# Second attention's head norm: two tiles' squares summed at once in two column groups, inverse roots held as two rounded parts

## Chip, cores and metric

The kernel runs on one core of a Trainium2 chip. The metric is the device time of one execution in microseconds (us); three executions of the kernel before are given with their median.

## What is computed

Two transformer blocks in sequence over 512 tokens and 16 meta tokens (528 rows) of width 1024, in fp32. The first block (gated delta rule, short convolution, gated feed-forward) is not touched. The second has two layers: sparse attention with an MLP, then the attention that the change is in (`fox_attention`) with an MLP. That attention needs keys, values and forget gates from one normalization of the residual and queries from another, and each head (64 wide, 16 heads) of the keys and of the queries is normalized by itself:

```python
def rms_norm(x, g):
    xf = x.astype(jnp.float32)
    y = xf * lax.rsqrt(jnp.mean(xf * xf, axis=-1, keepdims=True) + EPS)
    return (y * g.astype(jnp.float32)).astype(x.dtype)

def shared_kv(h, w_kv, f_bias, k_gain):
    k, v, fl = jnp.split(h @ w_kv, [B_W, 2 * B_W], axis=-1)
    k = rms_norm(k.reshape(B, T, B_HEADS, HEAD_DIM), k_gain)
    v = v.reshape(B, T, B_HEADS, HEAD_DIM)
    log_f = jax.nn.log_sigmoid(fl.astype(jnp.float32) + f_bias.astype(jnp.float32))
    c = jnp.cumsum(log_f, axis=1).transpose(0, 2, 1)
    ...
def fox_attention(h, w_q, q_gain, w_out, k, v, c):
    q = rms_norm((h @ w_q).reshape(B, T, B_HEADS, HEAD_DIM), q_gain)
    ...
```

## The kernel before

Data lie with features on the partitions: a tile is 128 features (two heads) by 528 tokens, so 8 tiles hold the keys and 8 the queries. Products with fp32 weights are made from two rounded parts of each operand (hi and lo, both fp32r): hi x hi, hi x lo, lo x hi. A **block** is one output tile: its weights are 128 x 1024 floats, loaded by SyncE's queue, split into hi by ScalarE (`split_hi`, L474) and lo by GpSimd (`split_lo`, L482), and multiplied on TensorE (`products`, L518) in 48 products, 3 parts x 8 rows of tiles x 2 halves of 264 tokens. Weight slots and PSUM accumulators are double: the weights of block j+1 are split while block j is multiplied, once block j-1 is done, and block j+2 may start when block j has been evicted.

The stage is written out by hand, one function for each engine (`pe_fox`, `act_fox`, `dve_fox`, `pool_fox`), each a loop over 25 blocks j; what stands in the code behind block j runs behind it in that engine's queue. Engines meet at semaphores: `f_sq` (squares made), `f_used` (sums made), `f_root`, `f_inv`, `f_spread`, `f_app` (tile normalized), `acc_free` (block evicted), `block_done` (block multiplied).

- Block 0 gives the forget gates, blocks 1 to 8 the keys (tiles 0 to 7), 9 to 16 the queries (tiles 8 to 15), 17 to 24 the values.
- VectorE evicts block j (L2651, times the row norm) and, for j < 8, makes one lo part of the second normalized input (`low`, L789) and one step of the forget-gate series (`dve_forget`, L2584 to L2621).
- ScalarE splits weights, squares tile n behind block j = n+2 (`square`, L2540, into one of two buffers `fox_sq`), and takes the roots of eight tiles' sums at j=10 and j=18 (`roots`, L2544).
- TensorE sums the squares of tile n behind block n+2 (`sums`, L2476): a product with a window of 16 columns that puts the two heads' sums into rows 2m and 2m+1 of PSUM and adds zero to the others, in fp32, for the two halves of the tokens.
- VectorE inverts the roots of eight tiles (`inverse`, L2630, in rows 0 to 15 of the otherwise zero `fox_inv`).
- TensorE spreads a tile's two rows over 128 partitions (`spreads`, L2485), in fp32 with a 0/1 matrix `fox_spread`: tiles 0 to 7 in blocks 11 to 14 and tiles 8 to 15 in blocks 19 to 22, an even one in the middle of a block (`midway`) and the odd one behind it.
- VectorE normalizes the tile with the result (`apply`, L2636). `spreads(n)` waits until tile n-1 has been normalized.

Behind the stage runs the attention. Three of its TensorE lines serve for comparison in what follows: L2250 (`scores`), L2282 (`turn`, a transposition, over all columns) and L2315 (`values`), where an fp32 product with 64 weight columns goes in turn to PSUM partitions 0 to 63 and 64 to 127:

```python
for hh in range(2):
    col = (p if fox else p // 4) * P + 64 * hh
    n = ROWS[kb + x]
    at2 = (hh * nk + x) * rows
    mm = pe.matmul(ps[64 * hh:64 * hh + 64, VALUE_BANK + t // 4, at:at + rows],
                   v[0:n, kb + x, col:col + 64], ptr[TURN["turn", j, i] % 4][0:n, at2:at2 + rows],
                   start=(kb + x == 0), stop=(kb + x == t))
```

Of the kernel before, what the change touches and what calls it, by code (L numbers as in the profile page):

```python
# [17 lines left out]
F32 = mybir.dt.float32  # L18
F32R = mybir.dt.float32r
BF16 = mybir.dt.bfloat16  # L20
ALU = mybir.AluOpType
ACT = mybir.ActivationFunctionType
AX = mybir.AxisListType

P = 128
# [3 lines left out]
T = NMETA + SEQ  # L29
HT = T // 2  # L30
# [26 lines left out]
def num(b):  # L57
    return b.c + 2 * b.i
# [56 lines left out]
def wait(e, sem, value):  # L115

    if isinstance(value, int) and value <= 0:
        return
    e.wait_ge(sem, value)
# [32 lines left out]
def build_program(nc, io):  # L152
# [9 lines left out]
    def region(start):  # L162
        pos = [start]

        def sb(name, shape, dt=F32):
            n = 2 if dt == BF16 else 4
            for s in shape[1:]:
                n *= s
            n = -(-n // 32) * 32
            off = pos[0]  # L170
            pos[0] += n
            return place(name, shape, dt, off)

        sb.pos = pos
        return sb
# [11 lines left out]
    ident = keep("ident", [P, P])  # L187
    ones = keep("ones", [P, P])
    win128 = keep("win128", [P, 31])
    win64 = keep("win64", [P, 30])  # L190
# [3 lines left out]
    eps = keep("eps", [P, 1])  # L194
# [98 lines left out]
    assert r2.pos[0] <= nc.sbuf_usable_end, r2.pos[0]  # L293
    rf = region(phase_at + 8 * F)
    fox_sq = [rf(f"fox_sq{u}", [P, T]) for u in range(2)]
    fox_root = rf("fox_root", [16, T])
    fox_inv = rf("fox_inv", [P, T])
    fox_spread = rf("fox_spread", [P, 8 * P])
    assert rf.pos[0] <= phase_at + 16 * F
    rs = region(phase_at + 24 * F)  # L300
    fox_sp = [rs(f"fox_sp{i}", [16, T]) for i in range(5)]
# [2 lines left out]
    bias = rdsa("bias", [C, NCH, T])  # L304
# [36 lines left out]
    ps = nc.alloc_psum_tensor("ps", [P, 8, 512], F32)  # L341
# [27 lines left out]
    def both(name):  # L369
# [23 lines left out]
    f_sq, f_used, f_root, f_inv, f_spread, f_app = map(sem, (  # L393
        "fox_square", "fox_square_used", "fox_root", "fox_inverse", "fox_spread", "fox_normalized"))
# [29 lines left out]
    def pair_of(b, rows=P):  # L424

        return ps[0:rows, b:b + 2, 0:HT]

    def two(ap):
        return ap.rearrange("p (h t) -> p h t", h=2)
# [9 lines left out]
    def tile_at(buf, m, n=T, off=0):  # L439
        step = TS if buf is qkv or buf is oacc else T  # L440
        return buf[:, bass.ds(m * step + off, n)]
# [111 lines left out]
    def stage_at(u):  # L553
        return stage[:, u * T:(u + 1) * T]
# [1912 lines left out]

    def pe_fox(pe):

        def sums(n):  # L2470
            m = n % 8
            pe.wait_ge(f_sq, n + 1)
            if n == 8:
                pe.wait_ge(f_root, 1)
            for h in range(2):
                mm = pe.matmul(ps[0:16, 4 + h, 0:HT], win64[:, 14 - 2 * m:30 - 2 * m],  # L2476
                               fox_sq[n % 2][:, h * HT:(h + 1) * HT], start=(m == 0), stop=(m == 7))
            mm.then_inc(f_used, 1)

        def spreads(n):  # L2480
            m = n % 8
            pe.wait_ge(f_inv, n // 8 + 1)
            wait(pe, f_app, n)
            for h in range(2):
                mm = pe.matmul(ps[:, 6 + h, 0:HT], fox_spread[:, m * P:(m + 1) * P], fox_inv[:, h * HT:(h + 1) * HT],  # L2485
                               start=True, stop=True)
            mm.then_inc(f_spread, 1)

        for j in range(25):
            x = (xbh, xbl) if 9 <= j <= 16 else (xah, xal)  # L2490
            first = dict(fresh=4, sums=pe_sums()) if j == 0 else dict(fresh=5) if j == 9 else {}
            n = 2 * (j - 11) if 11 <= j <= 14 else 8 + 2 * (j - 19) if 19 <= j <= 22 else None
            if n is not None:
                first["midway"] = lambda pe: spreads(n)
            products(pe, Blk(FOX + j, 0), *x, KT, **first)
            if j == 1:
                pe.wait_ge(acc_free, FOX + 1)
                for c in range(NCH):
                    mm = pe.matmul(ps[0:ROWS[c], 7, c:c + 1], rstd[0:1, c * C:ENDS[c]], ones[0:1, 0:1],
                                   start=True, stop=True)  # L2500
                mm.then_inc(f_turn, 1)
            if 2 <= j <= 17:
                sums(j - 2)
            if n is not None:
                spreads(n + 1)
            if j >= 18:
                fox_values(pe, j - 18)
# [25 lines left out]
    def act_fox(act):  # L2533
        root = act_root()

        def square(n):
            m = n % 8
            act.wait_ge(acc_free, FOX + n + 2)
            wait(act, f_used, n - 1)
            act.activation(fox_sq[n % 2][:, :], tile_at(pf, m if n < 8 else 16 + m), ACT.Square).then_inc(f_sq, 1)  # L2540

        def roots(i):
            act.wait_ge(f_used, 8 * (i + 1))
            act.activation(two(fox_root[:, :]), pair_of(4, 16), ACT.Sqrt, bias=eps[0:16, 0:1], scale=1.0 / 64  # L2544
                           ).then_inc(f_root, 1)

        def raw(m):
            b = Blk(FOX + 17 + m, 0)
            act.wait_ge(block_done, num(b) + 1)
            act.wait_ge(acc_free, num(b))  # L2550
            act.activation(two(stage_at(m % 2)), acc(b), ACT.Copy).then_inc(acc_free, 1)

        for j in range(25):
            split_hi(act, Blk(FOX + j + 1, 0))
            if j == 0:
                root(act)
            if j < 8:
                split_residual(act, j, 6, xbh, False)
            if j == 2:
                act.wait_ge(f_turn, 1)  # L2560
                act.activation(fox_tok[:, 0:4], ps[0:C, 7, 0:4], ACT.Copy)
                act.activation(fox_tok[0:ROWS[4], 4:5], ps[0:ROWS[4], 7, 4:5], ACT.Copy)
                act.wait_ge(sp_abs, 2)
                act.activation(fox_sp[0][:, :], lfneg[:, :], ACT.Abs)
                act.drain()
                act.activation(fox_sp[1][:, :], fox_sp[0][:, :], ACT.Exp, scale=-1.0).then_inc(sp_exp, 1)
            if 2 <= j <= 17:
                if j == 10:
                    roots(0)
                square(j - 2)  # L2570
            if j == 18:
                roots(1)
            if j >= 18:
                raw(j - 18)
            if j >= 19:
                store(act, j - 19)
            if j == 19:
                act.activation(rowvec[0:1, 7:8], eps[0:1, 0:1], ACT.Exp)
        raw(7)
# [44 lines left out]
    def dve_fox(dve):  # L2624
        root, low, forget = dve_root(), lows(5, 6, xbh, xbl), dve_forget(dve)

        def inverse(i):
            wait(dve, f_spread, 8 * i)
            dve.wait_ge(f_root, i + 1)
            dve.reciprocal(fox_inv[0:16, :], fox_root[:, :]).then_inc(f_inv, 1)  # L2630

        def apply(n):
            x = tile_at(pf, n if n < 8 else 8 + n)
            k = 3 if n < 8 else 4
            dve.wait_ge(f_spread, n + 1)
            dve.scalar_tensor_tensor(two(x), two(x), headgain[:, k:k + 1], pair_of(6), ALU.mult, ALU.mult  # L2636
                                     ).then_inc(f_app, 1)

        for j in range(17):
            b = Blk(FOX + j, 0)  # L2640
            if j == 0:
                root(dve)
            dve.drain()
            dve.wait_ge(block_done, num(b) + 1)
            dve.wait_ge(acc_free, num(b))
            if j == 0:
                dve.tensor_tensor(two(lfneg[:, :]), acc(b, 16), two(rstd[0:16, :]), ALU.mult).then_inc(acc_free, 1)
                dve.drain()
            else:
                x = tile_at(pf, j - 1 if j < 9 else j + 7)  # L2650
                dve.tensor_tensor(two(x), acc(b), two(rstd[:, :]), ALU.mult).then_inc(acc_free, 1)  # L2651
            if j < 8:
                low(dve, j)
                next(forget)
            if j == 8:
                dve.memset(fox_inv[:, :], 0.0)
                dve.tensor_copy(fox_spread[:, :].rearrange("p (k n) -> p k n", n=64),
                                ident[:, 0:16].unsqueeze(2).broadcast_to([P, 16, 64]))
                dve.drain()
            if j == 9:  # L2660
                inverse(0)
            if j == 10:
                apply(0)
            if 11 <= j <= 14:
                apply(2 * (j - 11) + 1)
                if j < 14:
                    apply(2 * (j - 11) + 2)
        inverse(1)
        for n in range(8, 16):
            apply(n)  # L2670
# [348 lines left out]
```

## Times and profile before

| | us |
|---|---|
| three executions | 2874.48, 2880.0, 2881.43 |
| median | 2880.0 |
| the profiled execution | 2881.1 |
| its span, first to last instruction | 2879.1 |
| TensorE busy in the span | 2684.5 (93%) |
| VectorE, ScalarE, GpSimd busy | 1389.8, 1019.5, 1085.3 |
| mean granted TensorE clock | 0.966 |

The profile comes from one execution. It has one record for each instruction; an fp32 matmul has two TensorE records, an fp32r matmul one. TensorE's records overlap, since they last until a result has left the array: how much time an instruction takes of the engine is read from the distance of the starts, not from its duration. The stage of the change lies between about 2170 and 2344 us.

### The profile page before, as it was taken

What the parts mean: (1) busy time and instruction counts of PE and PEld (TensorE: products, weight loads), DVE (VectorE), ACT (ScalarE), POOL (GpSimd) and SP (SyncE); (2) the same over time, 40 slices, a digit from 0 to 9 for tenths busy, and PEclk for the clock granted to TensorE, in tenths of its full rate; (3) what the DMA queues carried; (4) which work ended last, traced back from release to release, by engine and by line L of the source; (5) the groups of instructions that cost most, each with busy time, mean ns of one, the idle gap of its engine ahead of it and who ended that gap; (6) DMA issues with size and microseconds to landing.
All of it is one profiled execution on the core that took longest, in us unless ns stands there. A gap on an engine that the chain in (4) does not pass through costs nothing.

```text
span 2879.1 us, 48582 instructions
## 1 busy us (share of the span) xinstructions
PE 2684.5 (93%) x17811; PEld 2317.2 (80%) x17811; DVE 1389.8 (48%) x2068; ACT 1019.5 (35%) x1763; POOL 1085.3 (38%) x564
## 2 busy tenths in 40 slices
PE   6985887889999999999889899999999999999998
PEld 6974887868987778888778669999998886777876
DVE  2664566633212663233678656354367224545432
ACT  4772222233244242222523574222233256422222
POOL 3421333314444434444446214444444311444443
PEclk8997888899999999999999999999999999999999
DMA  2210000012222233223211002222222210223322
GB/s 97 91 55 6 12 10 11 13 60 88 90 92 95 88 96 95 93 90 95 95 52 54 21 2 81 88 88 90 91 88 74 66 45 2 68 94 95 95 88 94
DMA packets 88891, 197.91 MB, mean 69 GB/s; under 512 B 38172, under 2 KB 40270, under 8 KB 88760
## 3 DMA queue, kind: packets, MB, share of 16 engines
q1 hardware_dynamic: 84964, 192.72, 21.7%
q10 hardware_dynamic: 3796, 3.38, 0.4%
q8 instruction: 89, 1.46, 0.2%
q14 instruction: 42, 0.34, 0.0%
HBM read 192.24 MB, written 3.82 MB: 68 GB/s over the span
## 4 chain that ended last, share of the span: by engine, by line
issue 53%; POOL 13%; PE 5%; POOLq 3%; DVE 3%; DVEq 1%; ACT 1%; ACTq 0%
POOL wl L482 12%; PE ps L518 3%; POOLq L2220 2%; DVE work L2123 1%; DVE top L2120 1%; PE ps L1876 1%; POOL xbl L2229 1%; POOLq L130 0%; POOLq L2228 0%; POOLq L2217 0%; PE ps L881 0%; PE ps L893 0%; PE ps L2250 0%; DVEq L619 0%; DVEq L2121 0%
## 5 line engine op out<-in xcount | busy, mean ns | idle before, releaser
L482 POOL TENSOR_TENSOR wl<-wraw,wh 128x1024 fp32r<-128x1024 f32 x353 | 876.1, 2482 | 1210.6 <-ACT wh L474 1210.5
L474 ACT ACTIVATE wh<-wraw 128x1024 fp32r<-128x1024 f32 x353 | 372.5, 1055 | 575.6 <-PE ps L518 487.6
L518 PE MATMUL ps<-xah,wh 128*128 128x264 f32 (+1 forms) x2672 | 500.2, 328 | 25.3 <-ACT xah L847 14.2
L518 PE MATMUL ps<-xah,wl 128*128 128x264 f32 (+1 forms) x2672 | 488.0, 323 | 0.0
L518 PE MATMUL ps<-xal,wh 128*128 128x264 f32 (+1 forms) x2672 | 486.2, 322 | 0.0
L518 PEld LDWEIGHTS ps<-xah,wh 128*128 128x128 f32 x2672 | 405.4, 189 | 79.5 <-issue 23.3
L518 PEld LDWEIGHTS ps<-xah,wl 128*128 128x128 f32 x2672 | 403.8, 189 | 41.4 <-issue 0.8
L518 PEld LDWEIGHTS ps<-xal,wh 128*128 128x128 f32 x2672 | 401.7, 188 | 40.7
L666 DVE TENSOR_TENSOR res<-res,stage 128x512 f32 (+3 forms) x112 | 81.9, 731 | 442.0 <-ACT stage L582 442.0
L518 PE MATMUL ps<-xbh,wh 128*128 128x264 f32 (+1 forms) x1392 | 274.0, 337 | 13.6 <-POOL wl L482 13.0
L518 PE MATMUL ps<-xbh,wl 128*128 128x264 f32 (+1 forms) x1392 | 269.5, 333 | 0.0
L518 PE MATMUL ps<-xbl,wh 128*128 128x264 f32 (+1 forms) x1392 | 269.5, 333 | 0.0
L518 PEld LDWEIGHTS ps<-xbh,wh 128*128 128x128 f32 x1392 | 217.4, 188 | 48.7 <-POOL wl L482 16.5
L582 ACT ACTIVATE stage<-ps 128x512 f32<-128x512 f32 (+1 forms) x136 | 81.9, 602 | 460.8 <-PE ps L518 460.8
L518 PEld LDWEIGHTS ps<-xbl,wh 128*128 128x128 f32 x1392 | 217.5, 188 | 27.4
L518 PEld LDWEIGHTS ps<-xbh,wl 128*128 128x128 f32 x1392 | 217.4, 188 | 27.4
L659 DVE TENSOR_SCALAR xbh<-stage 128x512 f32 (+3 forms) x102 | 147.6, 1447 | 18.2 <-issue 16.6
L661 DVE TENSOR_TENSOR xbl<-stage,xbh 128x512 f32 (+3 forms) x102 | 114.5, 1122 | 15.2 <-issue 1.0
L2406 DVE TENSOR_REDUCE rowmax<-ps 106x2 f32<-106x212 f32 (+2 forms) x96 | 68.0, 708 | 85.3 <-PE ps L2262 40.5
L2227 POOL CAST xbh<-ofull 128x528 fp32r<-128x528 f32 x16 | 10.0, 623 | 220.5 <-DVE ofull L2441 220.5
L1392 POOL TENSOR_TENSOR qkm<-qkm,tri 106x424 f32<-106x424 f32 x20 | 19.8, 1011 | 180.7 <-DVE qkm L1511 180.7
L2250 PE MATMUL ps<-pf 64*106 64x212 f32 (+5 forms) x384 | 69.1, 438 | 12.8 <-DVEq L418 8.9
(347 smaller groups left out, 3089.0 us busy)
## 6 DMA issues: line engine op xcount, KB each, us to landing
wraw<-in_w SPq DMA_DIRECT2D x353, 512.0 KB, 3.5
res<-in_x SPq DMA_DIRECT2D x4, 528.0 KB, 5.6
res<-in_x ACTq DMA_DIRECT2D x1, 2048.0 KB, 7.8
out<-res SPq DMA_DIRECT2D x1, 2048.0 KB, 6.9
block_in<-mt SPq DMA_DIRECT2D x120, 4.0 KB
xq<-block_out SPq DMA_DIRECT2D x120, 8.0 KB
block_out<-yy SPq DMA_DIRECT2D x20, 56.0 KB
cossin<-in_cossin ACTq DMA_DIRECT2D x1, 528.0 KB
```

What stands on the lines that cost most here:

```text
L474: act.activation(wh[:, s * DM:(s + 1) * DM], wraw[:, s * DM:(s + 1) * DM], ACT.Copy).then_inc(hi_done, 1)
L482: pool.tensor_tensor(wl[:, s * DM:(s + 1) * DM], wraw[:, s * DM:(s + 1) * DM], wh[:, s * DM:(s + 1) * DM].bitcast(F32), ALU.subtract).then ...
L518: mm = pe.matmul(ps[:, 2 * s + h, 0:width], ws[:, s * DM + kk * P:s * DM + (kk + 1) * P], x[:, at:at + width], start=(h not in [o[0] for o ...
L582: act.activation(shaped(out(j, u), live), acc(b, live=live), func, **more).then_inc(acc_free, 1)
L659: dve.tensor_scalar(hi, x, 1.0, None, ALU.mult)
L661: return dve.tensor_tensor(lo, x, hi.bitcast(F32), ALU.subtract)
L666: return dve.tensor_tensor(r, r, live_stage(u) if live else stage_at(u), ALU.add)
L1876: mm = pe.matmul(ps[0:ROWS[t], 4 + 2 * (n % 2) + x, 0:c], ix_zero[:, 2 * (m % 2) + hh, C * t:ENDS[t]], pf[:, 16 * T + o:16 * T + o + c], s ...
L2120: dve.max(top8[0:ROWS[t], 8 * t:8 * t + 8], work_of(t))
L2220: pool.drain()
L2250: pe.matmul(ps[0:rows, b + hh, 0:hi - lo], pf[half, q0:q0 + rows], pf[half, k0 + lo:k0 + hi], start=True, stop=False)
L2406: most = dve.tensor_reduce(rowmax[0:rows, n, 1 if k == LAST4 else 0, :], ps[0:rows, b:b + 2, 0:hi - lo], AX.X, ALU.max, negate=True)
```

## The change

Squares are summed for two tiles at once, behind every second block (j = 3, 5, ..., 17): tile 2p into PSUM partitions 0 to 31 and tile 2p+1 into partitions 32 to 63, with a window `fox_win` that is 32 columns wide (the old one, widened by 16 zero columns). Roots and inverses then take 64 rows, of which 16 carry sums. The inverse is kept in two fp32r parts, rounded in rows 0 to 63 and the rest in rows 64 to 127 of `fox_inv`; `fox_spread` becomes an fp32r 0/1 matrix that picks both parts of a head's row, so that one fp32r product spreads a tile's inverses. `square(n)` waits for the sums of the pair before its own.

```diff
+    fox_root = rf("fox_root", [64, T])
+    fox_inv = rf("fox_inv", [P, T], F32R)
+    fox_spread = rf("fox_spread", [P, 8 * P], F32R)
+    fox_win = rf("fox_win", [P, 46])
...
-        def sums(n):
-            m = n % 8
-            pe.wait_ge(f_sq, n + 1)
-            if n == 8:
+        def sums(pair):
+            m = pair % 4
+            pe.wait_ge(f_sq, 2 * pair + 2)
+            if pair == 4:
                 pe.wait_ge(f_root, 1)
             for h in range(2):
-                mm = pe.matmul(ps[0:16, 4 + h, 0:HT], win64[:, 14 - 2 * m:30 - 2 * m],
-                               fox_sq[n % 2][:, h * HT:(h + 1) * HT], start=(m == 0), stop=(m == 7))
+                for u in range(2):
+                    mm = pe.matmul(ps[32 * u:32 * u + 32, 4 + h, 0:HT], fox_win[:, 14 - 2 * m:46 - 2 * m],
+                                   fox_sq[u][:, h * HT:(h + 1) * HT], start=(m == 0), stop=(m == 3))
             mm.then_inc(f_used, 1)
...
-            if 2 <= j <= 17:
-                sums(j - 2)
+            if 2 <= j <= 17 and j % 2:
+                sums((j - 3) // 2)
...
         def square(n):
-            wait(act, f_used, n - 1)
+            wait(act, f_used, n // 2)
...
         def roots(i):
-            act.wait_ge(f_used, 8 * (i + 1))
-            act.activation(two(fox_root[:, :]), pair_of(4, 16), ACT.Sqrt, bias=eps[0:16, 0:1], scale=1.0 / 64
+            act.wait_ge(f_used, 4 * (i + 1))
+            act.activation(two(fox_root[:, :]), pair_of(4, 64), ACT.Sqrt, bias=eps[0:64, 0:1], scale=1.0 / 64
...
         def inverse(i):
-            dve.reciprocal(fox_inv[0:16, :], fox_root[:, :]).then_inc(f_inv, 1)
+            dve.reciprocal(fox_root[:, :], fox_root[:, :])
+            dve.drain()
+            dve.tensor_copy(fox_inv[0:64, :], fox_root[:, :])
+            dve.drain()
+            dve.tensor_tensor(fox_inv[64:128, :], fox_root[:, :], fox_inv[0:64, :].bitcast(F32), ALU.subtract
+                              ).then_inc(f_inv, 1)
...
             if j == 0:
                 root(dve)
+                dve.memset(fox_win[:, 30:46], 0.0)
+                dve.tensor_copy(fox_win[:, 0:30], win64[:, :])
...
             if j == 8:
-                dve.memset(fox_inv[:, :], 0.0)
-                dve.tensor_copy(fox_spread[:, :].rearrange("p (k n) -> p k n", n=64),
-                                ident[:, 0:16].unsqueeze(2).broadcast_to([P, 16, 64]))
+                picks = fox_spread[:, :].rearrange("p (m u k n) -> p u m k n", u=2, k=2, n=64)
+                for u in range(2):
+                    hi, lo = (ident[:, at:at + 8].rearrange("p (m k) -> p m k", k=2).unsqueeze(3).broadcast_to(
+                        [P, 4, 2, 64]) for at in (32 * u, 64 + 32 * u))
+                    dve.tensor_tensor(picks[:, u, :, :, :], hi, lo, ALU.add)
                 dve.drain()
```

TensorE's queue behind blocks 3 and 4, before (`win` is the 16-column window, `xah`, `xal`, `wh` and `wl` the hi and lo parts of input and weights):

```order
L518 MATMUL ps<-xal,wh 128x264 x8
L2476 MATMUL ps<-fox_sq_165,win_61 16x264 [waits fox_square]
L2476 MATMUL ps<-fox_sq_165,win_61 16x264
L518 MATMUL ps<-xah,wh 128x264 [waits acc_free,lo_done]
L518 MATMUL ps<-xah,wh 128x264 x7
L518 MATMUL ps<-xah,wl 128x264 x8
L518 MATMUL ps<-xal,wh 128x264 x8
L518 MATMUL ps<-xah,wh 128x264 x8
L518 MATMUL ps<-xah,wl 128x264 x8
L518 MATMUL ps<-xal,wh 128x264 x8
L2476 MATMUL ps<-fox_sq_164,win_61 16x264 [waits fox_square]
L2476 MATMUL ps<-fox_sq_164,win_61 16x264
```

and the same place now, where line numbers are those of the changed kernel (L519 is the products, L2478 the sums):

```order
L519 MATMUL ps<-xal,wh 128x264 x8
L2478 MATMUL ps<-fox_sq_164,fox_win 32x264 [waits fox_square]
L2478 MATMUL ps<-fox_sq_165,fox_win 32x264
L2478 MATMUL ps<-fox_sq_164,fox_win 32x264
L2478 MATMUL ps<-fox_sq_165,fox_win 32x264
L519 MATMUL ps<-xah,wh 128x264 [waits acc_free,lo_done]
L519 MATMUL ps<-xah,wh 128x264 x7
L519 MATMUL ps<-xah,wl 128x264 x8
L519 MATMUL ps<-xal,wh 128x264 x8
L519 MATMUL ps<-xah,wh 128x264 x8
L519 MATMUL ps<-xah,wl 128x264 x8
L519 MATMUL ps<-xal,wh 128x264 x8
```

Two matmuls behind each block became four behind every second, alternating between the buffers and so between the column groups; behind block 4 the next block follows at once.

VectorE's queue from the eviction of block 8 (the first row) to the first `apply`, before:

```order
L2651 TENSOR_TENSOR pf<-ps,rstd 128x528 [waits acc_free,block_done]
L2656 MEMSET fox_inv 128x528
L2657 COPY fox_spread<-ident 128x1024
L2651 TENSOR_TENSOR pf<-ps,rstd 128x528 [waits acc_free,block_done]
L2630 RECIPROCAL fox_inv<-fox_root 16x528 [waits fox_root]
L2651 TENSOR_TENSOR pf<-ps,rstd 128x528 [waits acc_free,block_done]
L2636 SCALAR_TENSOR_TENSOR pf<-pf,headgain,ps 128x528 [waits fox_spread]
```

and now:

```order
L2660 TENSOR_TENSOR pf<-ps,rstd 128x528 [waits acc_free,block_done]
L2669 TENSOR_TENSOR fox_spread<-ident 128x4x128 x2
L2660 TENSOR_TENSOR pf<-ps,rstd 128x528 [waits acc_free,block_done]
L2632 RECIPROCAL fox_root<-fox_root 64x528 [waits fox_root]
L2634 CAST fox_inv<-fox_root 64x528
L2636 TENSOR_TENSOR fox_inv<-fox_root,fox_inv 64x528
L2660 TENSOR_TENSOR pf<-ps,rstd 128x528 [waits acc_free,block_done]
L2643 SCALAR_TENSOR_TENSOR pf<-pf,headgain,ps 128x528 [waits fox_spread]
```

The fill and the copy became two additions, and between the reciprocal and block 10's eviction stand two more instructions.

## Rows read from the trace of the kernel before

**Rows 1.** The page, parts 1 and 2: busy time, granted clock by slice.

```profile
PE 2684.5 (93%) x17811; PEld 2317.2 (80%) x17811; DVE 1389.8 (48%) x2068; ACT 1019.5 (35%) x1763; POOL 1085.3 (38%) x564
...
PEclk8997888899999999999999999999999999999999
```

**Rows 2.** The stage: length, busy PE, PEld, DVE, ACT, POOL (instructions), clock, DMA.

```profile
2172.50:2344.00 171.50, 171.50 (x1270) 155.90 (x1270) 64.55 (x66) 54.20 (x92) 63.08 (x27) 1.00 0.23 72
```

**Rows 3.** Timeline of TensorE, two plain blocks' first products (start, duration, instruction).

```profile
2131.18 1.15 PE L518 MATMUL ps<-xbh,wh 128*128 128x264 f32 x8
...
2137.02 1.15 PE L518 MATMUL ps<-xbh,wh 128*128 128x264 f32 x8
```

**Rows 4.** Timeline around the first two tiles' sums.

```profile
2177.93 1.13 PE L518 MATMUL ps<-xal,wh 128*128 128x264 f32 x8
...
2178.99 1.06 PE L2476 MATMUL ps<-fox_sq,win 128*16 128x264 f32 x4
2179.10 0.71 DVE L2651 TENSOR_TENSOR pf<-ps,rstd 128x528 f32<-128x528 f32 x1 [5.23 <-PE ps L518]
...
2180.75 0.63 ACT L2540 ACTIVATE fox_sq<-pf 128x528 f32<-128x528 f32 x1
...
2186.11 0.71 DVE L2651 TENSOR_TENSOR pf<-ps,rstd 128x528 f32<-128x528 f32 x1 [2.53 <-PE ps L518]
```

**Rows 5.** Groups of instructions from 2170 to 2340: sums and spreads.

```profile
L2485 PE MATMUL ps<-fox_inv,fox_spread 128*128 128x264 f32 x64 | 17.3, 392 | 0.0
...
L2476 PE MATMUL ps<-fox_sq,win 128*16 128x264 f32 x64 | 17.0, 389 | 0.0
```

**Rows 6.** Timeline of TensorE in the attention, then a cut of it.

```profile
2355.30 1.50 PE L2315 MATMUL ps<-ptr,vtok 106*64 106x106 f32 x28
...
2357.33 0.70 PE L2282 MATMUL ps<-ident,prob 104*106 104x104 f32 x6
...
2355.30 0.31 PE L2315 MATMUL ps<-ptr,vtok 106*64 106x106 f32 x2
```

**Rows 7.** Timeline of VectorE, evictions of blocks 11 and 14.

```profile
2243.17 0.71 DVE L2651 TENSOR_TENSOR pf<-ps,rstd 128x528 f32<-128x528 f32 x1 [2.15 <-PE ps L518]
...
2269.60 0.71 DVE L2651 TENSOR_TENSOR pf<-ps,rstd 128x528 f32<-128x528 f32 x1 [2.15 <-PE ps L518]
```

**Rows 8.** Timeline of VectorE from block 4's eviction to block 8's, one GpSimd row.

```profile
2193.12 0.71 DVE L2651 TENSOR_TENSOR pf<-ps,rstd 128x528 f32<-128x528 f32 x1 [2.10 <-PE ps L518]
...
2201.37 2.58 POOL L482 TENSOR_TENSOR wl<-wraw,wh 128x1024 fp32r<-128x1024 f32 x1 [3.82 <-ACT wh L474]
...
2201.79 4.27 DVE L2605 SCALAR_TENSOR_TENSOR fox_sp<-fox_sp,fox_sp 16x528 f32<-16x528 f32 x3
2207.19 0.71 DVE L2651 TENSOR_TENSOR pf<-ps,rstd 128x528 f32<-128x528 f32 x1 [1.14 <-PE ps L518]
...
2219.31 0.42 DVE L2618 CAST decay_row<-lfneg 16x528 bf16<-16x528 f32 x1
2219.81 0.70 DVE L2621 TENSOR_TENSOR lfneg<-lfneg,decay_row 16x528 f32<-16x528 f32 x1
...
2222.47 0.71 DVE L2651 TENSOR_TENSOR pf<-ps,rstd 128x528 f32<-128x528 f32 x1 [0.19 <-issue]
```

**Rows 9.** Timeline: preparation of the spread, both inversions, and the spreads behind them.

```profile
2223.24 0.50 DVE L2656 MEMSET fox_inv<- 128x528 f32 x1
2223.65 1.75 DVE L2657 COPY fox_spread<-ident 128x1024 f32<-128x1024 f32 x1
2228.25 0.71 DVE L2651 TENSOR_TENSOR pf<-ps,rstd 128x528 f32<-128x528 f32 x1 [2.85 <-PE ps L518]
2231.40 3.44 DVE L2630 RECIPROCAL fox_inv<-fox_root 16x528 f32<-16x528 f32 x1 [2.45 <-ACT fox_root L2544]
...
2239.17 1.05 PE L2485 MATMUL ps<-fox_inv,fox_spread 128*128 128x264 f32 x4
...
2293.41 3.44 DVE L2630 RECIPROCAL fox_inv<-fox_root 16x528 f32<-16x528 f32 x1 [8.11 <-ACT fox_root L2544]
2301.92 1.05 PE L2485 MATMUL ps<-fox_inv,fox_spread 128*128 128x264 f32 x4
```

More of the change, by code:

```diff
@@ L295, in build_program @@
     fox_sq = [rf(f"fox_sq{u}", [P, T]) for u in range(2)]
-    fox_root = rf("fox_root", [16, T])
-    fox_inv = rf("fox_inv", [P, T])
-    fox_spread = rf("fox_spread", [P, 8 * P])
+    fox_root = rf("fox_root", [64, T])
+    fox_inv = rf("fox_inv", [P, T], F32R)
+    fox_spread = rf("fox_spread", [P, 8 * P], F32R)
+    fox_win = rf("fox_win", [P, 46])
     assert rf.pos[0] <= phase_at + 16 * F
```

## The prediction

> **What bounds the kernel now.** I read the page's first two parts, then the stage that the change touches. TensorE is busy for 93% of the span and the granted clock is 9 tenths or more from the ninth slice on, so a stage is judged by whether TensorE ever waits in it [rows 1]. In the second attention's projections (2172.5 to 2344.0) it never does: 171.50 us busy of 171.50, granted clock 1.00 (that is 2.4 GHz), while VectorE works 64.55, ScalarE 54.20 and GpSimd 63.08 us there [rows 2]. So every microsecond that leaves TensorE's queue in this stage leaves the stage, as long as the other engines keep up with shorter blocks; and a microsecond added on VectorE costs nothing until something on TensorE waits for it.
>
> The unit of the stage is one weight block: 48 one-pass products. Two blocks with nothing else between them follow each other in 5.84 us (first products at 2131.18 and 2137.02), which is 0.122 us a product [rows 3].
>
> **The sums.** From j=2 to 17 each block is followed by one tile's sums. The evictions, which start when a block's products end, are then 7.01 us apart (2179.10, 2186.11) [rows 4]: a tile's sums cost 7.01 - 5.84 = 1.17 us, sixteen of them 18.7. Four records make them up, two passes for each of the two fp32 matmuls (64 records for 32 matmuls [rows 5]); 0.89 of the 1.17 is these four passes at 0.22 each, and 0.28 is paid once for the group. The gap ahead of it shows: the eight products from 2177.93 should be through at 2177.93 + 8 x 0.122 = 2178.90, and the sums begin at 2178.99 [rows 4].
> The change issues the same 32 matmuls, but four at a time, every second block (the order above). If the two column groups work side by side, a pair of tiles costs four slots of 0.22 and one 0.28, say 1.18 with the stagger. The trace of before has a witness: L2315 in the attention writes PSUM partitions 0 to 63 and 64 to 127 in turn, with 106 rows of weights (all four row groups), in fp32. There two records start in the same hundredth of a microsecond, and 28 records of 106 columns are through between 2355.30 and about 2356.6, 0.047 us each, where L2282, also fp32 and 106 columns but over the full width, needs (0.70 - 0.25) / 5 = 0.09 each [rows 6]. Full overlap, then, for 64-column groups. I take it for 32-column ones too. Gain: 8 x (2 x 1.17 - 1.18) = **9.3 us**. The other bound is no overlap: eight passes of 0.22 plus 0.28 is 2.06 a pair, a gain of 8 x 0.28 = 2.2 us.
> The Trainium skill ("TensorEngine Tiling (Array Packing)", Tiling Modes, Key Properties) says that a change of tiling mode drains the array but a change of tile within a mode does not; by this rule the drain is paid at both ends of each group, eight groups where there were sixteen, and not between the two column groups, so the sum would be mine. The 0.09 us gap of rows 4 agrees with the first half, the twin starts of rows 6 with the second.
>
> **The spreads.** Between the evictions of blocks 11 and 14 lie three stretches of (2269.60 - 2243.17) / 3 = 8.81 us, each with one block, one tile's sums and two spreads [rows 7]. A spread costs (8.81 - 5.84 - 1.17) / 2 = 0.90 us: again four records of 0.22 for two fp32 matmuls [rows 5]. As fp32r operands each half is one pass over 128 weight columns and 264 moving ones, exactly the shape and type of the products: 2 x 0.122 = 0.24. Sixteen spreads save 16 x 0.66 = **10.5 us**. The bounds are close here; both ends are rows of this stage.
>
> **VectorE's new work.** (a) `fox_win` at j=0: a fill and a 30-column copy, each under the 0.50 us of the fill of `fox_inv` [rows 9], since both touch far less. Behind them queues only block 0's eviction, for which TensorE waits behind block 1. Nothing, at most 0.5 us. (b) At j=8 the 0.50 fill and 1.75 copy go (the copy took 1.75 because it began while GpSimd was at work) and two adds of 128x512 come, about 0.70 each like any two-input operation [rows 8, 9]. Nothing. (c) `inverse`: after the 3.44 us reciprocal come a conversion (about 0.42, the nearest being the cast) and a subtraction (about 0.70) [rows 8, 9], with drains 1.3 us. With block 9 ending at 2228.15 (its eviction starts at 2228.25) the reciprocal ended at 2234.84 and the first spread came at 2239.17: 4.3 us of slack [rows 9]. Now the first spread comes 1.17 + 5.84 + 2.92 = 9.93 us after block 9, as block 10 has no sums any more, and the inverse is ready 6.69 + 1.3 = 8.0 after it. 1.9 us of cover remain; nothing is paid, and if this cover fails TensorE waits at j=11's midway. The second `inverse` ended at 2296.85 for a spread at 2301.92; 3.8 us remain [rows 9]. Nothing.
> (d) Block 10's eviction queues behind the longer inverse by about 1 us; only block 12 needs the bank. Nothing.
>
> **Where cover gets thin.** The forget-gate series runs on VectorE between the evictions. From the eviction of block 4 (2193.12) to that of block 8 (2222.47) pass 29.35 us, of which only 1.14 and 0.19 are idle [rows 8]: 28.0 us of work. TensorE took 28.04 for these four blocks and will take 4 x 5.84 + 2 x 1.18 = 25.7. VectorE reaches block 8's eviction 2.3 us late, ends it 3.0 late, and the square takes 0.63 more [rows 4]. The pair sums need it 5.84 after block 8's end: 2.2 us to spare. Evictions and weight splits have a block of slack more. So **nothing** is charged.
>
> **Sum.** 9.3 + 10.5 = 19.8 us. Made against the profiled execution it is 2881.1 - 19.8 = 2861.3; the runs' median lies 1.1 us under that execution, and the forecast is for a median: 2880.0 - 19.8 = **2860.2 us**. After the stage everything shifts as one, since weights are fetched only two blocks ahead.
>
> **Rivals.**
> *The columns don't overlap* (only the spreads gain in full): 10.5 + 2.2 = 12.7, time 2867.3. For it: 32-column groups with two 128-row moving streams of 264 columns appear nowhere in this trace. Against: rows 6. Chance 0.09.
> *VectorE comes late.* A two-input operation that starts while GpSimd subtracts waits for its end: L2621 takes 0.70, and three L2605 of the same size took 4.27 instead of 2.1 with a GpSimd subtraction under way from 2201.37 to 2203.95 [rows 8]. One such wait (2.1 us) already falls in most iterations; with blocks of 5.84 us and a VectorE that lags, a second one can fall into j=5, 6 or 7 or on `inverse`'s subtraction. Two more would eat the 2.2 us and stall the fourth pair of sums by about 2; one on `inverse` stalls the first spread by 1.3. Time 2860.2 + 2 to 4 = 2862 to 2864. Chance 0.14. The Trainium skill ("SBUF — State Buffer", Who interferes with whom) states it as a rule, that the one who comes second blocks fully; by it every late iteration risks a whole GpSimd instruction, and the time is that of this rival. The stretched L2605 agrees with the rule.
> *Each change of column group costs what the group's edges cost* (slower than before). The passes of rows 6 alternate between the groups, so a pair of tiles has seven changes. If each cost 0.28 and nothing overlapped, that is 56 x 0.28 = 15.7 us against the 12.7 gained: 2883.0. It is slower than before from 0.23 us a change, by over 0.3% from 0.38. Rows 6 show changes at under 0.01 us; only 32 columns behaving unlike 64 would bring it. Chance 0.02.
> *The spread keeps its two passes.* Then only 9.3 are gained, 2870.7. The products' 0.122 us with the same type speaks against it. Chance 0.03.
>
> **How the numbers follow.** Forecast 0.70; the remaining 0.02 is for a cause that I don't see, on either side. Likeliest: 2860.2. The runs of before reach from 5.5 under to 1.4 over their median, so the forecast alone spans 2854.7 to 2861.6; the late VectorE reaches 2864 and the missing overlap 2867.3 + 1.4. Range 2854.5 to 2868.7. A measurement of this kernel tells a change of 0.3% or 8.6 us from none: faster is below 2871.4, which all cases but the third rival and the unseen cause meet. Faster 0.94, same 0.04, slower 0.02.
>
> **What would show it.** Right: 32 spread records instead of 64, about 0.12 us apart; sum records starting in twos; evictions after blocks with sums 7.0 us behind the last and after blocks without 5.84; at block 14's eviction (2269.60 before) a lead of 12 x 1.17 - 6 x 1.18 + 7 x 0.66 = 11.6 us; TensorE still without idle time in the stage, which ends near 2324. Wrong: sum groups of 2 us; an idle stretch ahead of the sums of j=9 or the spread of j=11; a granted clock under 1.00 anywhere in the stage; or a stage 20 us shorter with the end not 20 us earlier, which would mean the attention behind it had waited for something else.

## The result and the profile after

The change takes 2858.4 us (median of 4 runs, 2856.6 to 2859.7) against 2880.2 us before (4 runs in the same comparison, 2874.5 to 2881.4). The ratio is 0.9928 with a 95% interval of 0.9911 to 0.9945. That is 21.7 us less, where 19.8 were forecast. The granted clock of the page is the share of TensorE's full clock, 2.4 GHz, that it got.

The page of the changed kernel, parts 1 and 2, beside [rows 1]:

```profile
span 2854.8 us, 48528 instructions
...
PE 2655.9 (93%) x17779; PEld 2299.2 (81%) x17779; DVE 1393.1 (49%) x2074; ACT 1020.1 (36%) x1763; POOL 1084.5 (38%) x564
...
PEclk8997888999999999999999999999999999999999
```

TensorE has 32 instructions fewer: sixteen spreads of four records became sixteen of two. VectorE has 6 more.

The whole span can't size the effect, since it is 24.3 us shorter here. So I measured the stage by itself, from the reciprocal of the row norm on VectorE, with which it opens, to the first fill of the row sums, with which the attention behind it begins. First the two ends before:

```profile
2166.24 3.45 DVE L761 RECIPROCAL rstd<-rstd 128x528 f32<-128x528 f32 x1 [2.05 <-ACT rstd L744]
...
2344.11 0.08 DVE L2445 MEMSET rowsum<- 106x24 f32 x1 [12.03 <-PE ps L518]
```

and after, with the new preparation of the window between them:

```profile
2161.66 3.45 DVE L762 RECIPROCAL rstd<-rstd 128x528 f32<-128x528 f32 x1 [2.05 <-ACT rstd L745]
2165.22 0.50 DVE L2651 COPY fox_win<-win 128x30 f32<-128x30 f32 x1
2165.22 0.07 DVE L2650 MEMSET fox_win<- 128x16 f32 x1
2165.89 0.69 DVE L2656 TENSOR_TENSOR lfneg<-ps,rstd 16x528 f32<-16x528 f32 x1 [0.17 <-issue]
...
2319.65 0.08 DVE L2446 MEMSET rowsum<- 106x24 f32 x1 [12.05 <-PE ps L519]
```

The stage shrank from 177.87 to 158.00 us, by **19.87**. Behind it the two executions agree within 0.2 us (535.0 and 535.1 to the end). The other 4.6 us of the span had been won before the stage opened (2166.24 against 2161.66), in code that both kernels share. The expectations below speak of the stage from block 0's eviction, 173.8 and 153.8 us; that measure makes the gain 0.2 larger (20.07), because the eviction itself starts 0.2 later behind the reciprocal. The table further down has both.

How the stage runs now, in VectorE's timeline (evictions of blocks 2 to 4 and 11 to 14, beside [rows 4] and [rows 7]):

```profile
2174.53 0.71 DVE L2660 TENSOR_TENSOR pf<-ps,rstd 128x528 f32<-128x528 f32 x1 [2.88 <-PE ps L519]
...
2180.36 0.71 DVE L2660 TENSOR_TENSOR pf<-ps,rstd 128x528 f32<-128x528 f32 x1 [1.35 <-PE ps L519]
...
2187.42 0.71 DVE L2660 TENSOR_TENSOR pf<-ps,rstd 128x528 f32<-128x528 f32 x1 [2.14 <-PE ps L519]
...
2232.06 0.71 DVE L2660 TENSOR_TENSOR pf<-ps,rstd 128x528 f32<-128x528 f32 x1 [2.15 <-PE ps L519]
...
2239.57 0.71 DVE L2660 TENSOR_TENSOR pf<-ps,rstd 128x528 f32<-128x528 f32 x1 [2.15 <-PE ps L519]
...
2245.88 0.71 DVE L2660 TENSOR_TENSOR pf<-ps,rstd 128x528 f32<-128x528 f32 x1 [2.15 <-PE ps L519]
...
2253.40 0.71 DVE L2660 TENSOR_TENSOR pf<-ps,rstd 128x528 f32<-128x528 f32 x1 [2.15 <-PE ps L519]
```

Between blocks 2 and 3 there are no sums: 5.83 us. Between 3 and 4 there is a pair's: 7.06. Farther on, a stretch with a pair's sums and two spreads is 7.51 and one with two spreads alone 6.31, where each was 8.81. A spread thus costs (6.31 - 5.84) / 2 = 0.24 us, and a pair's sums 1.20. At block 14's eviction the lead over the kernel before, counted from the opening of the stage, is (2269.60 - 2166.24) - (2253.40 - 2161.66) = 11.6 us, as forecast. TensorE's own timeline shows both kinds:

```profile
2180.26 1.08 PE L2478 MATMUL ps<-fox_sq,fox_win 128*32 128x264 f32 x8
2181.27 1.24 PE L519 MATMUL ps<-xah,wh 128*128 128x264 f32 x8
...
2228.71 0.40 PE L2487 MATMUL ps<-fox_inv,fox_spread 128*128 128x264 f32 x2
2228.95 1.13 PE L519 MATMUL ps<-xbh,wh 128*128 128x264 f32 x8
```

Eight records of sums take 1.01 us to the next block's start, as long as four did in [rows 4] (2178.99 to 2179.98). The two column groups overlap in full. Two spread records take 0.24.

### The profile page after: what moved, and what is told of

It reads as the page before. It is cut to its first block, busy times and chain, and to the rows that moved or that the text cites. A ratio compares the mean times of both kernels' runs of the same rounds, so it can differ in the third digit from the quotient of the medians.

```text
span 2854.8 us, 48528 instructions
## 1 busy us (share of the span) xinstructions
PE 2655.9 (93%) x17779; PEld 2299.2 (81%) x17779; DVE 1393.1 (49%) x2074; ACT 1020.1 (36%) x1763; POOL 1084.5 (38%) x564
## 4 chain that ended last, share of the span: by engine, by line
issue 53%; POOL 13%; PE 5%; POOLq 3%; DVE 3%; DVEq 1%; ACT 1%; ACTq 0%
POOL wl L483 12%; PE ps L519 3%; POOLq L2221 2%; DVE work L2124 1%; DVE top L2121 1%; PE ps L1877 1%; POOL xbl L2230 1%; POOLq L130 0%; POOLq L2229 0%; POOLq L2218 0%; PE ps L882 0%; PE ps L894 0%; PE ps L2251 0%; DVEq L620 0%; DVEq L2122 0%
## 5 line engine op out<-in xcount | busy, mean ns | idle before, releaser
L519 PE MATMUL ps<-xah,wh 128*128 128x264 f32 (+1 forms) x2672 | 498.9, 327 | 25.2 <-ACT xah L848 14.2
L519 PE MATMUL ps<-xah,wl 128*128 128x264 f32 (+1 forms) x2672 | 488.2, 323 | 0.0
L519 PE MATMUL ps<-xal,wh 128*128 128x264 f32 (+1 forms) x2672 | 486.7, 322 | 0.0
L519 PEld LDWEIGHTS ps<-xah,wh 128*128 128x128 f32 x2672 | 405.1, 189 | 77.4 <-issue 21.4
L519 PEld LDWEIGHTS ps<-xah,wl 128*128 128x128 f32 x2672 | 404.0, 189 | 41.3 <-issue 0.8
L519 PEld LDWEIGHTS ps<-xal,wh 128*128 128x128 f32 x2672 | 402.5, 188 | 40.7
L519 PE MATMUL ps<-xbh,wh 128*128 128x264 f32 (+1 forms) x1392 | 272.1, 335 | 13.5 <-POOL wl L483 12.9
L519 PE MATMUL ps<-xbl,wh 128*128 128x264 f32 (+1 forms) x1392 | 269.5, 333 | 0.0
L519 PE MATMUL ps<-xbh,wl 128*128 128x264 f32 (+1 forms) x1392 | 269.4, 333 | 0.0
L519 PEld LDWEIGHTS ps<-xbh,wh 128*128 128x128 f32 x1392 | 216.9, 188 | 47.1 <-POOL wl L483 16.4
L519 PEld LDWEIGHTS ps<-xbl,wh 128*128 128x128 f32 x1392 | 217.5, 188 | 27.4
L519 PEld LDWEIGHTS ps<-xbh,wl 128*128 128x128 f32 x1392 | 217.4, 188 | 27.4
L1393 POOL TENSOR_TENSOR qkm<-qkm,tri 106x424 f32<-106x424 f32 x20 | 19.8, 1010 | 177.5 <-DVE qkm L1512 177.5
```

The lines of the kernel that those rows point to most:

```text
L519: mm = pe.matmul(ps[:, 2 * s + h, 0:width], ws[:, s * DM + kk * P:s * DM + (kk + 1) * P], x[:, at:at + width], start=(h not in [o[0] for o ...
```

## The experiments

The table has the stage of each kernel from its profile, by both measures, and what the rows say of the gain. "Gain" is 177.87 less the first column.

| kernel | from the reciprocal | from block 0's eviction | gain |
|---|---|---|---|
| before | 177.87 | 173.8 | |
| sums alone | 168.46 | 164.2 | 9.4 |
| spreads alone | 167.49 | 163.4 | 10.4 |
| spreads, pairs in one column group | 165.16 | 161.1 | 12.7 |
| the same, window of 128 columns | 162.64 | 158.4 | 15.2 |
| the change | 158.00 | 153.8 | 19.9 |
| the change, other order of groups | 158.13 | 153.9 | 19.7 |
| the change, VectorE 3.4 us late | 164.12 | 159.9 | 13.8 |
| the change, VectorE 1.5 us late | 159.41 | 155.2 | 18.5 |
| four column groups | 154.98 | 150.8 | 22.9 |
| four groups, forget step later | 154.79 | 150.6 | 23.1 |

### The sums alone

Against the changed kernel (so are the edits below, where nothing else is said):

```diff
-            dve.reciprocal(fox_root[:, :], fox_root[:, :])
-            dve.drain()
-            dve.tensor_copy(fox_inv[0:64, :], fox_root[:, :])
-            dve.drain()
-            dve.tensor_tensor(fox_inv[64:128, :], fox_root[:, :], fox_inv[0:64, :].bitcast(F32), ALU.subtract
-                              ).then_inc(f_inv, 1)
+            dve.reciprocal(fox_inv[0:64, :], fox_root[:, :]).then_inc(f_inv, 1)
```

with `fox_inv` and `fox_spread` back in fp32 and the second half of `fox_inv` zero. Expected:

> The sums in pairs and two column groups, the spreads as before (two fp32 matmuls, one-part inverse). Stage length, from block 0's eviction to the attention's first fill of the row sums, was 173.8 us before and is 153.8 with the whole change. My theory (TensorE time alone counts): 9.3 us of the gain is here, so a stage of 164.5 us and a time near 2871. Rival (the sums gain nothing by themselves, since only shorter spreads were felt): stage 173.8, time 2880.

Measured: stage 164.2, time 2872.7 us, ratio 0.9973 (0.9963 to 0.9982). The gain of 9.4 is the predicted 9.3.

### The spreads alone

Against the kernel before (the preparation of `fox_inv` and `fox_spread` in their new type is left out here):

```diff
-            dve.reciprocal(fox_inv[0:16, :], fox_root[:, :]).then_inc(f_inv, 1)
+            dve.reciprocal(fox_root[:, :], fox_root[:, :])
+            dve.drain()
+            dve.tensor_copy(fox_inv[0:16, :], fox_root[:, :])
+            dve.drain()
+            dve.tensor_tensor(fox_inv[64:80, :], fox_root[:, :], fox_inv[0:16, :].bitcast(F32), ALU.subtract
+                              ).then_inc(f_inv, 1)
```

> The spreads as one fp32r product with a two-part inverse, the sums as before, a tile behind each block. My theory: 16 x 0.66 = 10.5 us, so a stage of 163.3 us and a time near 2869.5; VectorE has its old slack, so no wait before any sums. Rival (part of the 20 us came from elsewhere, and the spreads have less): a stage over 165.

Measured: stage 163.4, time 2869.8 us, ratio 0.9966 (0.9952 to 0.9980). 10.4 us, and 9.4 + 10.4 = 19.8: the parts add up to the whole, so neither takes cover from the other.

### Pairs of tiles in one column group

```diff
             for h in range(2):
                 for u in range(2):
-                    mm = pe.matmul(ps[32 * u:32 * u + 32, 4 + h, 0:HT], fox_win[:, 14 - 2 * m:46 - 2 * m],
-                                   fox_sq[u][:, h * HT:(h + 1) * HT], start=(m == 0), stop=(m == 3))
+                    n = 2 * m + u
+                    mm = pe.matmul(ps[0:16, 4 + h, 0:HT], win64[:, 14 - 2 * n:30 - 2 * n],
+                                   fox_sq[u][:, h * HT:(h + 1) * HT], start=(n == 0), stop=(n == 7))
...
```

> The spreads as one fp32r product, and the sums behind every second block as now, but both tiles of a pair in the old 16 columns, so that no two column groups are at work. This parts overlap from grouping. My theory: only the edges of eight groups go, 8 x 0.28 = 2.2 us on top of the spreads' 10.5, stage 161.1, time near 2867; groups of 8 records 0.22 us apart, about 2.06 us in all. Rival (the gain of the sums is that TensorE's stream is broken eight times less, not the overlap): stage 153.8 as with the whole change.

Measured: stage 161.1, time 2866.8 us, ratio 0.9955 (0.9938 to 0.9972). TensorE's timeline:

```profile
2183.98 1.96 PE L2478 MATMUL ps<-fox_sq,win 128*16 128x264 f32 x8
2185.87 1.24 PE L518 MATMUL ps<-xah,wh 128*128 128x264 f32 x8
```

Eight records take 1.89 us here and 1.01 in two groups. Of the sums' 9.4 us, 2.3 come from half as many groups of instructions (12.7 against the 10.4 of the spreads alone) and 7.2 from the overlap (19.9 against 12.7). This would have been the whole kernel's time (2867) if the first rival had come true.

### The order of the groups

```diff
-            for h in range(2):
-                for u in range(2):
+            for u in range(2):
+                for h in range(2):
                     mm = pe.matmul(ps[32 * u:32 * u + 32, 4 + h, 0:HT], fox_win[:, 14 - 2 * m:46 - 2 * m],
```

> The whole change, but within a pair both halves of one tile come first and then both halves of the other, so that the program changes the column group once instead of three times. Theory A (matmuls start in the order of the program, and one may start early only beside the one ahead of it): the first tile's four passes run alone but for the last, seven slots of 0.22 in place of four, 8 x 0.67 = 5.3 us more, stage 159.1. Theory B (each column group works through a queue of its own): nothing changes, stage 153.8.

Measured: stage 153.9, one run of 2858.1 us. Theory A is refuted and the time is that of theory B: all four passes of one tile stand ahead of those of the other in the program, and the eight records still take as long.

```profile
2181.59 1.09 PE L2478 MATMUL ps<-fox_sq,fox_win 128*32 128x264 f32 x8
2182.62 1.24 PE L519 MATMUL ps<-xah,wh 128*128 128x264 f32 x8
```

A cut of the same timeline up to 2181.70 has two records that start together:

```profile
2181.59 0.43 PE L2478 MATMUL ps<-fox_sq,fox_win 128*32 128x264 f32 x2
```

Within one column group two passes start 0.22 us apart (eight in 1.89 us above), so these two belong to different groups, and the second tile's first pass began before the first tile's were through. The records don't name their group, so a queue for each group is an inference from this and not seen.

### VectorE made late

```diff
                 next(forget)
+                if j == 7:
+                    dve.drain()
+                    dve.reciprocal(fox_sp[4][:, :], fox_sp[0][:, :])
```

> The whole change with one more reciprocal (3.44 us, into a scratch buffer) on VectorE behind block 7's work, which moves the eviction of block 8 and the square of tile 7 back. In the changed kernel that square ended at 2218.64 and the sums that need it began at 2218.85. Theory (the fourth pair's sums are now the tightest place, with some 0.2 us of cover): TensorE idles about 3.3 us ahead of the sums of j=9, stage 157.1 us against 153.8. Rival (VectorE's lateness is harmless, since evictions have a block of slack): stage 153.8.

Measured: stage 159.9, one run of 2866.4 us. The wait is where the theory had it, and as long, but the stage grew by 6.1 us and not by 3.3. First what TensorE waited for, then its timeline, then stretches around it (length, busy PE, PEld, DVE, ACT and POOL, granted clock, DMA):

```profile
PE ps L2478 <- ACT fox_sq L2542: 3.3, 1, 3.3
```

```profile
2226.02 1.98 PE L2478 MATMUL ps<-fox_sq,fox_win 128*32 128x264 f32 x8 [3.27 <-ACT fox_sq L2542]
2227.93 2.13 PE L519 MATMUL ps<-xbh,wh 128*128 128x264 f32 x8
2229.85 1.97 PE L519 MATMUL ps<-xbh,wl 128*128 128x264 f32 x8
```

```profile
2218.00:2222.50 4.50, 4.50 (x40) 4.50 (x38) 4.30 (x3) 0.12 (x1) 4.00 (x2) 1.00 0.19 40
2222.50:2226.00 3.50, 0.25 (x3) 0.04 (x1) 3.36 (x4) 0.67 (x2) 0.00 (x0) 0.90 0.27 103
2226.00:2228.00 2.00, 1.98 (x9) 0.63 (x9) 1.20 (x2) 1.98 (x2) 1.01 (x1) 0.50 0.00 0
2228.00:2230.00 2.00, 2.00 (x9) 2.00 (x10) 1.04 (x1) 1.45 (x3) 1.85 (x2) 0.50 0.00 0
2230.00:2232.00 2.00, 2.00 (x11) 2.00 (x10) 2.00 (x1) 0.00 (x0) 1.10 (x1) 0.50 0.71 188
2232.00:2234.00 2.00, 2.00 (x18) 2.00 (x17) 1.53 (x3) 0.00 (x0) 0.00 (x0) 0.96 0.18 74
```

TensorE had been idle for 3.3 us, and from then to about 2232 it ran at 0.50, the lower of its two levels (1.2 GHz in place of 2.4). In that time eight products take 1.92 us in place of 0.97, so about 6 us at this level do the work of 3, which accounts for the missing 2.8 us. Whether the clock fell for the idle or with it by chance was still open, hence the next run.

The other traces help with this question too. Every one of the eleven has an idle of 8.9 to 9.0 us near 1600 us and several of 1.2 to 1.7 us from about 1778 us on. The first brings the clock to 0.50, the others leave it at 1.00. From the changed kernel, the first and what follows it, then an idle of 1.55 us and what follows that:

```profile
1596.30:1605.20 8.90, 0.03 (x1) 0.00 (x0) 7.94 (x25) 2.35 (x9) 0.00 (x0) 0.77 0.00 1
1605.30:1611.00 5.70, 4.17 (x18) 2.07 (x19) 1.38 (x5) 3.25 (x9) 0.00 (x0) 0.50 0.01 3
...
1776.90:1778.45 1.55, 0.00 (x0) 0.03 (x1) 1.41 (x1) 0.00 (x0) 0.84 (x1) 1.00 0.00 0
1778.45:1785.00 6.55, 6.55 (x50) 6.42 (x51) 4.35 (x3) 1.76 (x2) 2.40 (x1) 1.00 0.26 80
```

### VectorE late by less

```diff
+                if j == 7:
+                    dve.drain()
+                    dve.reciprocal(fox_sp[4][:, 0:220], fox_sp[0][:, 0:220])
```

> As the run with the late VectorE, with a reciprocal of 220 columns in place of 528, 1.5 us instead of 3.44. There an idle of 3.3 us ahead of the sums of j=9 made the stage 6.1 us longer, and the granted clock stood at 0.50 for some 6 us behind it. Theory (the idle is paid once as idle and, when it is long enough to lower the clock, again in slow products): this idle is 1.3 us, the clock stays at 1.00 and the stage is 153.8 + 1.3 = 155.1. Rival (the second half of the cost is VectorE's lateness, which goes on behind the sums): about twice the idle again, stage near 156.4 with a clock of 1.00.

Measured: stage 155.2, one run of 2862.1 us. A wait of 1.3 us is there, and the clock stays at 1.00 in all three stretches around it:

```profile
2224.50 1.08 PE L2478 MATMUL ps<-fox_sq,fox_win 128*32 128x264 f32 x8 [1.34 <-ACT fox_sq L2542]
```

```profile
2219.00:2224.00 5.00, 4.16 (x35) 3.94 (x33) 4.74 (x4) 0.20 (x1) 3.60 (x2) 1.00 0.30 100
2224.00:2226.00 2.00, 1.50 (x12) 0.87 (x13) 1.68 (x3) 1.98 (x3) 0.53 (x1) 1.00 0.05 20
2226.00:2232.00 6.00, 6.00 (x52) 6.00 (x51) 4.42 (x3) 2.21 (x4) 3.45 (x2) 1.00 0.29 87
```

It costs 1.4 us, the wait itself. So the excess of the run before isn't VectorE's lateness, which costs nothing here beyond what TensorE waits. The wait of 3.3 us cost nearly twice its length, and the excess is the clock. Each of the two waits was run once.

### Four column groups

```diff
-                    mm = pe.matmul(ps[32 * u:32 * u + 32, 4 + h, 0:HT], fox_win[:, 14 - 2 * m:46 - 2 * m],
+                    mm = pe.matmul(ps[64 * h + 32 * u:64 * h + 32 * u + 32, 4, 0:HT], fox_win[:, 14 - 2 * m:46 - 2 * m],
...
-            act.activation(two(fox_root[:, :]), pair_of(4, 64), ACT.Sqrt, bias=eps[0:64, 0:1], scale=1.0 / 64
+            act.activation(fox_root[:, :], ps[:, 4, 0:HT], ACT.Sqrt, bias=eps[:, 0:1], scale=1.0 / 64
...
-            dve.tensor_copy(fox_inv[0:64, :], fox_root[:, :])
+            for h in range(2):
+                dve.tensor_copy(fox_inv[0:64, h * HT:(h + 1) * HT], fox_root[64 * h:64 * h + 64, :])
...
```

> The two halves of the tokens get column groups of their own too: four groups of 32 columns, output partitions 64h+32u, one PSUM bank; roots and reciprocals take 128 rows of 264 numbers. If four groups overlap like two, a pair's sums cost two slots of 0.22 and 0.28 plus a stagger, 0.75 us instead of 1.17, and TensorE's own work in the stage falls by 3.4 us to 150.4. Theory (VectorE is at its limit between blocks 4 and 9): 1.3 us of the gain come before the sums of j=9 and only 0.2 can be had there, so TensorE waits about 1.1 us at that place and the stage is 151.5. Rival (no limit): 150.4. Rival (only two moving streams can be read at a time): 153.8.

Measured: stage 150.8, time 2858.4 us, ratio 0.9928 (0.9913 to 0.9943). All four groups overlap:

```profile
2186.10 0.65 PE L2478 MATMUL ps<-fox_sq,fox_win 128*32 128x264 f32 x8
2186.68 1.24 PE L519 MATMUL ps<-xah,wh 128*128 128x264 f32 x8
```

Eight records in 0.58 us instead of 1.01, and 3.0 us off the stage. The theory of the wait missed: I gave it 1.1 us, and only the weight load ahead of the sums of j=9 waited, for 0.3 us. My error was to put VectorE at its limit from block 4 on. It is there only from block 6 on: in the change it still waited 0.55 us for that block's products, and here no such wait is left. First the change, then this run:

```profile
2200.29 0.71 DVE L2660 TENSOR_TENSOR pf<-ps,rstd 128x528 f32<-128x528 f32 x1 [0.55 <-PE ps L519]
```

```profile
2205.33 0.71 DVE L2663 TENSOR_TENSOR pf<-ps,rstd 128x528 f32<-128x528 f32 x1
```

Block 8's eviction thus follows block 4's after 29.4 us here and 29.8 in the change, and block 4's is itself 0.4 us earlier in the stage. VectorE follows 0.9 of the 1.3 us, and with the 0.2 of cover some 0.2 is left to wait for.

### Four groups and a later forget step

Against the run before:

```diff
                 low(dve, j)
+            if j < 7 or j == 15:
                 next(forget)
```

> Four column groups as in the run before, and the last step of the forget-gate series (the scan and the three bf16 parts, 5 us of VectorE) moved from block 7 to block 15, where VectorE is idle. Theory: the wait ahead of the sums of j=9 is gone, the whole 3.4 us are had, stage 150.4, time near 2855. Rival (the wait was never there): the same stage as in the run before.

Measured: stage 150.6, time 2855.1 us (5 runs), ratio 0.9921 (0.9908 to 0.9935). It is the fastest by median, but its stage is only 0.2 us under the run before, which is what was left to wait for; the 3 us between the two medians are within both intervals (the profiled executions differ by 6.3 us ahead of the stage), so they show no effect. Its worth is cover: block 8's eviction starts 5.4 us behind block 7's, where in the change it is 9.94, so VectorE is no longer late there.

### Sums at full width

Against the run with pairs in one column group (`fox_win` is widened to 142 columns, which is left out here):

```diff
-                    mm = pe.matmul(ps[0:16, 4 + h, 0:HT], win64[:, 14 - 2 * n:30 - 2 * n],
+                    mm = pe.matmul(ps[:, 4 + h, 0:HT], fox_win[:, 14 - 2 * n:14 - 2 * n + P],
```

> As the run with one column group (sums behind every second block, spreads in fp32r), but with a window of 128 columns, zero but for two, so that the sums use the array at full width like the products. Theory (the 0.28 us edge of a group of sums is the change between narrow and full-width use): groups of 8 records cost 1.78 us instead of 2.06, stage 161.1 - 2.2 = 158.9. Rival (the edge comes with any fp32 group, or with the wait for the squares): stage 161.1.

Measured: stage 158.4, one run of 2863.9 us.

```profile
2182.71 1.94 PE L2479 MATMUL ps<-fox_sq,fox_win 128*128 128x264 f32 x8
2184.30 1.32 PE L519 MATMUL ps<-xah,wh 128*128 128x264 f32 x8
```

The group is not preceded by a gap, and the eight groups together cost 165.16 - 162.64 = 2.5 us less than in 16 columns, 0.31 each, although each weight load is eight times as wide. The rival is refuted, since these are fp32 groups with the same wait. The edge of a group of sums (0.28 us in the prediction) is the change between narrow and full-width use. The Trainium skill ("TensorEngine Tiling (Array Packing)", Tiling Modes, Key Properties) has the rule that changing the tiling mode drains the array; this run agrees, and prices the way there and back at 0.3 us. That the array is drained meanwhile can't be read from the records.

## Why the prediction was right

- **TensorE's time is the stage's time.** Right: TensorE has no wait in the stage after the change either, and what left its queue left the stage (19.8 forecast, 19.87 measured). The stage after, as in [rows 2]:

```profile
2165.90:2319.60 153.70, 153.70 (x1255) 147.33 (x1255) 70.81 (x73) 55.19 (x92) 62.18 (x27) 1.00 0.27 83
```

- **The sums, 9.3 us.** Right: 9.4 alone. The inference from the 64-column groups of [rows 6] to 32 columns held, and the pairs in one group show that the overlap carries 7.2 of it.
- **The spreads, 10.5 us.** Right: 10.4 alone.
- **VectorE's new work, nothing.** Right, and `inverse` was ready in time: its subtraction ended at 2226.84 and the spread began at 2228.71, 1.9 us of cover as computed. The window's preparation cost block 0's eviction 0.2 us, for which nobody waited.
- **Where cover gets thin.** The place was right and the size was off. The timelines of VectorE, of GpSimd's weight splits (POOL) and of ScalarE's square:

```profile
2207.32 2.40 POOL L483 TENSOR_TENSOR wl<-wraw,wh 128x1024 fp32r<-128x1024 f32 x1 [3.39 <-ACT wh L475]
2207.92 2.36 DVE L790 SCALAR_TENSOR_TENSOR xbl<-res,gains,xbh 128x528 fp32r<-128x528 f32 x1
...
2214.36 2.40 POOL L483 TENSOR_TENSOR wl<-wraw,wh 128x1024 fp32r<-128x1024 f32 x1 [4.64 <-ACT wh L475]
2214.52 2.54 DVE L2620 CAST decay_row<-lfneg 16x528 bf16<-16x528 f32 x1
2217.24 0.71 DVE L2660 TENSOR_TENSOR pf<-ps,rstd 128x528 f32<-128x528 f32 x1 [0.19 <-issue]
...
2217.99 0.65 ACT L2542 ACTIVATE fox_sq<-pf 128x528 f32<-128x528 f32 x1 [3.70 <-DVE pf L2660]
```

  `low` (0.76 before) took 2.36 and the last cast (0.42) took 2.54, as each began while GpSimd was subtracting. In the kernel before one instruction of block 7's work was stretched like this (the scan, 3.27 us where it takes 1.25 in the change), now two are: the mechanism of the second rival, with one more such wait where the rival's price needs two. VectorE's work from block 4's eviction to block 8's came to 29.1 us, not 28.0, and it was idle for 0.7 us besides (0.55 of it waiting for block 6's products), which the sum put at nothing. So it began the eviction 29.8 - 25.7 = 4.1 us late (block 8's products ended just before ScalarE's next weight split began, at 2213.22), not 2.3. The square ended at 2218.64 and the sums began at 2218.85. Of the 2.2 us to spare, 0.2 were left. So the sum was right with little to spare. A further wait of 2.1 us would have stalled TensorE; the prediction had a chance for that and no working that excludes it, so that none fell is partly luck. Nor was the rival's price sure: I took a wait at its length, and the late runs show that one of 1.3 us costs 1.4 and one of 3.3 us costs 6.1. What one of 2 us costs was not run.
- **The other rivals.** No overlap and a costly change of group are refuted by the records of the change itself, the latter also by the run with the other order. The spread has one pass a half.
- **The end.** The time came out 1.8 us under the forecast's 2860.2. The stage gives the change 19.87 us of the 21.7 between the medians; the other 1.9 are none of its effect, and that they came out so small is luck. They are within what the part ahead of the stage does by itself: in the traces of this study the stage opens between 2161.2 and 2167.5 us, with the same instructions ahead of it.

## What to carry to other kernels

When one engine is busy through a whole stage, price a change by the distance of that engine's starts, not by durations, and then ask of every other engine how late it may come; here 20 us of gain left 0.2 us of cover at one place. Narrow fp32 sums that don't depend on each other belong in column groups of their own (up to four were measured), and gathered, since each group of narrow instructions between full-width ones pays 0.3 us here. Measure such a change by its stage in the trace when executions differ by more than the effect, and do one part alone: two parts of 9.4 and 10.4 that add up to 19.8, where both together give 19.87, leave no room for a third cause.

## What the runs showed of the hardware

- A change between full width and 16 columns and back costs 0.3 us for a group of sums; a window of 128 columns doesn't pay it, although its weight loads are eight times as wide.
- Four column groups of 32 columns, each with its own moving stream of 128 rows in fp32, run side by side: eight records of 264 columns in 0.58 us, against 1.01 in two groups and 1.89 in one.
- The order in the program doesn't matter for this: with all passes of one group ahead of the other's, the records take 1.03 us.
- In one run TensorE's granted clock fell from 1.00 to 0.50 late in an idle of 3.3 us and stayed there for about 6 us, in which it had plenty of work again; in another run an idle of 1.3 us left it at 1.00. The idles of 8.9 us and of 1.2 to 1.7 us in every trace agree.
- The two executions of the first comparison differ by 4.6 us ahead of the stage, with the same instructions. Between GpSimd's starts of the 25th and the 29th weight block, around the delta-rule stage, lie 461.97 us before (174.40 to 636.37) and 456.17 after (175.50 to 631.67). These 5.8 us are more than the whole difference. What varies there was not looked into.
